# A twentieth place for expert weights, made of two pieces of reused memory

## What is computed

```python
def grouped_moe(h, router_w, router_bias, w1, w3, w2):   # h: 256 x 1024
    scores = sigmoid(h @ router_w)                       # 256 x 16
    gates = the top 2 experts of the best of 4 groups, normalised
    for e in range(16):                                  # w1, w3: 1024 x 512, w2: 512 x 1024
        a = silu(t @ w1[e]) * (t @ w3[e])
        y = y + gates[:, e:e + 1] * (a @ w2[e])
for i in range(2):
    x = x + g1 * mixer(h)          # h = modulate(rms_norm(x))
    x = x + g2 * grouped_moe(h)    # h = modulate(rms_norm(x))
return rms_norm(x, final_g)
```

## Time and profile before

| | us |
|---|---|
| median of 3 runs | 1049.43 |
| the profiled execution, its own time | 1049.43 |
| its span, first to last instruction | 1047.6 |
| TensorE busy | 997.7 (95%) |
| layer 0: first and last product of the experts | 324.30 to 539 |
| layer 1: first and last product of the experts | 821.41 to 1032 |

### The profile page before, as it was taken

The page is one execution under the profiler, slowest core; times in us unless marked ns, Lnnn a source line. Parts: engine busy times, 40 slices in busy tenths (PEclk is TensorE's granted clock), DMA queues, the critical chain, the costliest instruction groups (busy, mean ns, idle before and its releaser), DMA issues.

```text
span 1047.6 us, 18346 instructions
## 1 busy us (share of the span) xinstructions
PE 997.7 (95%) x7709; PEld 602.5 (58%) x7709; DVE 564.1 (54%) x1192; ACT 188.5 (18%) x395; POOL 40.5 (4%) x83
## 2 busy tenths in 40 slices
PE   7999999999999999998999999999999999999794
PEld 4788567557775344443358866765878534444321
DVE  4669794868786223361235779572758622233112
ACT  4031001311233031011131110122123301110102
POOL 2100100010000000000010010001000000000000
PEclk9999999999999999999999999999999999999997
DMA  9999856297976999999999884628875599999991
GB/s 310 387 381 332 280 172 232 85 330 278 418 292 224 421 386 421 420 421 421 420 388 375 291 311 162 222 71 288 301 286 213 200 420 420 421 419 421 421 417 71
DMA packets 91883, 333.94 MB, mean 319 GB/s; under 512 B 5740, under 2 KB 6059, under 8 KB 66965
## 3 DMA queue, kind: packets, MB, share of 16 engines
q1 hardware_dynamic: 87937, 323.56, 79.3%
q0 software_dynamic: 2976, 7.19, 2.3%
q10 hardware_dynamic: 884, 1.97, 0.6%
HBM read 329.47 MB, written 1.05 MB: 316 GB/s over the span
## 4 chain that ended last, share of the span: by engine, by line
PE 78%; DVE 8%; DMA 6%; SPq 3%; issue 2%; ACT 1%; DVEq 0%; ACTq 0%
PE bank L833 76%; DMA ring<-in_moe_w_dram 4%; SPq L732 3%; DMA ring<-in_w_ada_dram 2%; PE bank L1345 1%; PE bank L1121 1%; DVE wide L2018 0%; DVE area L2014 0%; DVE wide L1807 0%; PE bank L1174 0%; DVE x L2234 0%; PE bank L895 0%; DVE area L2233 0%; DVE area L2210 0%; DVE wide L2019 0%
## 5 line engine op out<-in xcount | busy, mean ns | idle before, releaser
L833 PE MATMUL bank<-ring,hT 128*32 128x512 f32 (+3 forms) x1808 | 283.8, 555 | 9.8 <-DMA ring<-in_moe_w_dram 7.0
L833 PE MATMUL bank<-hT,ring 128*32 128x256 f32 (+1 forms) x2112 | 211.8, 380 | 0.1
L833 PEld LDWEIGHTS bank<-ring,hT 128*32 128x32 f32 (+2 forms) x1808 | 120.8, 134 | 144.8 <-issue 139.6
L833 PEld LDWEIGHTS bank<-hT,ring 128*32 128x32 f32 (+1 forms) x2112 | 157.6, 132 | 52.2 <-issue 5.5
L833 PE MATMUL bank<-ring,area 128*32 128x512 f32 (+1 forms) x744 | 117.8, 566 | 1.3 <-ACT area L1681 0.9
L833 PE MATMUL bank<-area 32*64 32x64 f32 (+5 forms) x648 | 89.1, 363 | 0.0
L1807 DVE SCALAR_TENSOR_TENSOR area<-ring,wide,area 128x512 f32<-128x512 f32 x114 | 85.3, 748 | 2.7
L2442 DVE TENSOR_TENSOR area<-bank,area 128x512 f32<-128x512 f32 x14 | 9.7, 691 | 130.4 <-PE bank L833 130.4
L833 PE MATMUL bank<-wide,hT 128*32 128x512 f32 (+1 forms) x376 | 75.1, 574 | 0.0
L833 PEld LDWEIGHTS bank<-ring,area 128*32 128x32 f32 (+1 forms) x744 | 43.6, 120 | 53.7 <-issue 48.6
L833 PEld LDWEIGHTS bank<-area 32*64 32x64 f32 (+4 forms) x648 | 37.9, 145 | 45.7 <-issue 44.4
(11 more groups left out here) (300 smaller groups left out, 1077.7 us busy)
## 6 DMA issues: line engine op xcount, KB each, us to landing
ring<-in_moe_w_dram SPq DMA_DIRECT2D x136, 1024.0 KB, 16.5
ring<-in_w_ada_dram SPq DMA_DIRECT2D x24, 2048.0 KB, 15.0
ring<-in_w_in_dram SPq DMA_DIRECT2D x24, 2048.0 KB, 12.3
wide<-in_moe_w_dram SPq DMA_DIRECT2D x32, 1024.0 KB, 12.8
cst<-in_moe_w_dram SPq DMA_DIRECT2D x13, 1024.0 KB, 14.9
area<-in_moe_w_dram SPq DMA_DIRECT2D x11, 1024.0 KB, 19.5
ring<-in_w_out_dram SPq DMA_DIRECT2D x4, 2048.0 KB, 8.5
ring<-in_w_br_h_dram SPq DMA_DIRECT2D x4, 1536.0 KB, 6.7
```

The lines of the kernel that those rows point to most:

```text
L833: return pe.matmul(dst, lhsT, rhs, start=start, stop=stop, skip_group_check=True)
```

## The change

One place more, `PIECES`, for both layers. It has two pieces of 1024 columns: the upper half of `hT`, and `area` from `AREA - 6 * W` to `AREA - 4 * W`. To free the first, `hg` becomes the lower 1024 columns in one piece; to free the second, `selh`, `sil`, and half of `yS` go (their values are written into `sel`, `act` and `actT`). The new place is appended to the end of `free` at the start of each layer's experts. Its first block waits for `p_part`; a block in it is loaded by two DMAs of 512 KB (128 x 4 KB) in place of one of 1 MB (128 x 8 KB), both on the place's one semaphore, and `half_row` picks the piece for each row of weights. To have a semaphore left for it, two early ones (`s_rates` and `s_tab`) become one.

```diff
-        hg = hT[:, :, 0:P]
+        hT_flat = hT[:, :, :].rearrange("p k n -> p (k n)")
+        hg = hT_flat[:, 0:ND * P].rearrange("p (k s) -> p k s", k=ND)
...
-        selh = region(NT * P).rearrange("p (t s) -> p t s", t=NT)
         selT = region(SEQ)
-        sil = region(FE)
         act = region(FE)
-        actT = region(FE).rearrange("p (f s) -> p f s", f=NF)
-        yS = region(D)
+        actT_flat = region(FE)
+        actT = actT_flat.rearrange("p (f s) -> p f s", f=NF)
+        yS = (region(W), actT_flat)
...
-        assert cut[0] <= AREA - 4 * W
+        assert cut[0] <= AREA - 6 * W
+        halves += [(hT_flat[:, ND * P:2 * ND * P], area[:, AREA - 6 * W:AREA - 4 * W])]
...
                         if L + 1 == DEPTH:
                             free.insert(12, (ROWS, None))
+                        free.append((PIECES, None))
...
+                    if u == PIECES:
+                        landings[u] += 16
                     plan[key] = halves[u], u, landings[u] + 16, [old]
...
+        def half_row(space, k, f):
+            if isinstance(space, tuple):
+                per = 2 * W // f
+                space, k = space[k // per], k % per
+            return space[:, k * f:(k + 1) * f]
...
+                    elif u == PIECES:
+                        sp.wait_ge(p_part, (L + 1) * NT)
...
+                    rows, f = ((NF if m == 2 else ND) // 2, D if m == 2 else FE)
+                    spaces = dst if isinstance(dst, tuple) else (dst,)
+                    count = rows // len(spaces)
+                    for i, space in enumerate(spaces):
+                        first = half * rows + i * count
+                        sp.dma_start(space.rearrange("p (k f) -> p k f", f=f),
+                                     t[name][L, experts[e], :, :].rearrange(order, p=P)[:, first:first + count, :])\
+                          .then_inc(landing, 16)
...
                 def rates_to_all(l):
                     if l == 0:
-                        pe.wait_ge(s_rates, 16 * 2)
+                        pe.wait_ge(s_rates_tab, 16 * 3)
...
-                    sc.activation(sil, bank[0][:, :], ACT.Silu).then_inc(a_sil, 1)
+                    sc.activation(act, bank[0][:, :], ACT.Silu).then_inc(a_sil, 1)
...
-                    dv.tensor_tensor(act, bank[1][:, :], sil, ALU.mult).then_inc(v_act, 1)
+                    dv.tensor_tensor(act, bank[1][:, :], act, ALU.mult).then_inc(v_act, 1)
...
-                    link(dv.tensor_tensor(selg[b], selg[b], selh, ALU.add))
+                    link(dv.tensor_tensor(selg[b], selg[b], sel, ALU.add))
```

More of the change, by code:

```diff
@@ L77 @@
 EXTRA = 2 * RING
-TABLE, TAIL, ROWS = EXTRA + 4, EXTRA + 5, EXTRA + 6
+TABLE, TAIL, ROWS, PIECES = EXTRA + 4, EXTRA + 5, EXTRA + 6, EXTRA + 7
 LAST = {(0, EXTRA): 3, (0, EXTRA + 1): 3, (0, EXTRA + 2): 1, (0, EXTRA + 3): 1, (1, EXTRA + 2): 3, (1, EXTRA + 3): 3}
@@ L408, in trunk_kernel @@
         mask = cst[:, C_MASK:C_MASK + NT * KEYS].rearrange("p (t n) -> p t n", t=NT)
-        slot_in = [sem(f"slot_in{u}") for u in range(ROWS + 1)]
+        slot_in = [sem(f"slot_in{u}") for u in range(PIECES + 1)]
         p_ada = sem("p_ada")
@@ L420, in trunk_kernel @@
         s_taps = sem("s_taps")
-        s_rates = sem("s_rates")
+        s_rates_tab = sem("s_rates_tab")
         a_dec = sem("a_dec")
@@ L691, in _ @@
             for n in range(2):
-                sp.dma_start(rates[32 * n:32 * n + 1, :], t["decay"][n:n + 1, :]).then_inc(s_rates, 16)
+                sp.dma_start(rates[32 * n:32 * n + 1, :], t["decay"][n:n + 1, :]).then_inc(s_rates_tab, 16)
             for L, kind, b, half in loads:
@@ L730, in _ @@
                     name, order = ("moe_w1", "moe_w3", "moe_w2")[m], "(p k) f -> p k f"
-                    part = slice(half * (NF if m == 2 else ND) // 2, (half + 1) * (NF if m == 2 else ND) // 2)
-                    sp.dma_start(dst.rearrange("p (k f) -> p k f", f=D if m == 2 else FE),
-                                 t[name][L, experts[e], :, :].rearrange(order, p=P)[:, part, :]).then_inc(landing, 16)
+                    rows, f = ((NF if m == 2 else ND) // 2, D if m == 2 else FE)
[6 more added lines that the diff above has]
+                          .then_inc(landing, 16)
                 elif L == 0 and (kind == "rest" or (kind == "in" and b * 4 < AHEAD)):
@@ L927, in spectrum @@
                         pe.wait_ge(v_kt, (l + 1) * 12)
-                        pe.wait_ge(s_tab, 16)
+                        pe.wait_ge(s_rates_tab, 16 * 3)
                     else:
@@ L1328, in up @@
                                 pe.wait_ge(landing, value)
-                                ws.append(w.rearrange("p (k f) -> p k f", f=FE))
+                                ws.append(w)
                         if which == 0 and k == 0:
@@ L1358, in down @@
                             pe.wait_ge(landing, value)
-                            ws.append(w.rearrange("p (k f) -> p k f", f=D))
+                            ws.append(w)
                         for h in range(2):
@@ L1388, in scatter @@
                             mm(bank[2 + 2 * tt + h][:, :], selT[:, tt * P:(tt + 1) * P],
-                               yS[:, h * W:(h + 1) * W], True, True).then_inc(p_sc, 1)
+                               yS[h], True, True).then_inc(p_sc, 1)
                 def next_filter(s, spot):
@@ L1465, in _ @@
                                 last = mm(bank[2 + 2 * tt + h][:, :], selT[:, tt * P:(tt + 1) * P],
-                                          yS[:, h * W:(h + 1) * W], True, True)
+                                          yS[h], True, True)
                         last.then_inc(X["x_sc"], 1)
@@ L1479, in _ @@
                 sc.dma_start(x[:, tt, :], t["x"][0, tt * P:(tt + 1) * P, :]).then_inc(s_x, 16)
-            sc.dma_start(cst[:, C_CT:C_IC], t["cst"][:, C_CT:C_IC]).then_inc(s_tab, 16)
+            sc.dma_start(cst[:, C_CT:C_IC], t["cst"][:, C_CT:C_IC]).then_inc(s_rates_tab, 16)
             sc.wait_ge(p_rows, 2)
@@ L1680, in _ @@
                     sc.wait_ge(p_actT, n + 1)
-                    sc.activation(actT[:, :, :].rearrange("p f s -> p (f s)"), bank[0][:, :], ACT.Copy)\
+                    sc.activation(actT_flat, bank[0][:, :], ACT.Copy)\
                       .then_inc(a_actT, 1)
@@ L1717, in _ @@
                             sc.dma_start(w1, rows_in("moe_w3", 0)).then_inc(X["x_in"], 16)
-                            sc.activation(sil, bank[0][:, :], ACT.Silu).then_inc(X["x_sil"], 1)
+                            sc.activation(act, bank[0][:, :], ACT.Silu).then_inc(X["x_sil"], 1)
                             sc.wait_ge(X["x_up"], i * 4 + 3)
@@ L1724, in _ @@
                             sc.activation(selT, bank[4][:, 0:SEQ], ACT.Copy)
-                            sc.activation(actT[:, :, :].rearrange("p f s -> p (f s)"), bank[5][:, :], ACT.Copy)\
+                            sc.activation(actT_flat, bank[5][:, :], ACT.Copy)\
                               .then_inc(X["x_aturn"], 1)
@@ L1731, in _ @@
                 sc.activation(stat[:, 10, 0:1], eps[:, :], ACT.Sqrt)
-                used = ((sil, actT[:, :, :].rearrange("p f s -> p (f s)")), (hT[:, 0:4, P:SEQ], hT[:, 4:ND, P:SEQ]))
+                used = ((act, area[:, 0:W]), (hT_flat[:, 0:W], hT_flat[:, W:2 * W]))
                 for tt in range(NT):
@@ L2349, in select @@
                                          ALU.is_equal, ALU.mult)
-                        last = dv.tensor_scalar(selh[:, tt, :], iota, where[:, s, NT + tt:NT + tt + 1],
+                        last = dv.tensor_scalar(sel[:, tt, :], iota, where[:, s, NT + tt:NT + tt + 1],
                                                 token[:, 3, tt:tt + 1], ALU.is_equal, ALU.mult)
                     link(last)
-                    link(dv.tensor_tensor(selg[b], selg[b], selh, ALU.add))
+                    link(dv.tensor_tensor(selg[b], selg[b], sel, ALU.add))
                     dv.tensor_scalar(sel, selg[b], 0.0, None, ALU.is_gt).then_inc(v_sel, 1)
@@ L2450, in _ @@
                         dv.wait_ge(p_down, n * 2 + h + 1)
[L2451 removed]
+                        dv.tensor_tensor(yS[h], bank[6 + h][:, :], g2b[:, cols], ALU.mult).then_inc(v_yS, 1)
                 accumulate(STEPS - 1)
@@ L2479, in _ @@
                             dv.wait_ge(X["x_up"], i * 4 + 4)
-                            dv.tensor_tensor(act, bank[1][:, :], sil, ALU.mult).then_inc(X["x_act"], 1)
+                            dv.tensor_tensor(act, bank[1][:, :], act, ALU.mult).then_inc(X["x_act"], 1)
                             dv.wait_ge(X["x_down"], i * 2 + 2)
@@ L2483, in _ @@
                                 cols = slice(h * W, (h + 1) * W)
-                                last = dv.tensor_tensor(yS[:, cols], bank[6 + h][:, :], g2b[:, cols], ALU.mult)
+                                last = dv.tensor_tensor(yS[h], bank[6 + h][:, :], g2b[:, cols], ALU.mult)
                             last.then_inc(X["x_yS"], 1)
```

6 lines of the change are left out of this document (2 added, 4 removed).

## The result

The kernel after takes 1043.36 us, the median of 5 runs (1042.17 to 1043.95), against 1049.43 before: a ratio of 0.9939, with a 95% interval of 0.9925 to 0.9954. The forecast was 1045.1; the direction was right, and the gain is 6.1 us in place of 4.3. The profiled span is 1041.6 us (before 1047.6), so 6.0 us are gone from it.

A forecast was written before the change was run, and what follows sets the result against it. The late-starting weight stream was taken to bound both layers' experts. Span 1047.6 - 2.2 (layer 0) - 2.1 (layer 1) = 1043.3, so 1045.1 us of time; own range 1043.8 to 1046.3, overall range 1043.3 to 1049.6.

The forecast's parts named there:

- What bounds the kernel: Both layers' expert parts: the weight stream, full at 420 GB/s but started late, sets the end through the last block's landing.
- The new place: Each layer's expert stream: one block loads in idle time before the first release, so later blocks land 2.49 us earlier.
- Price of the pieces: Blocks loaded as two 4 KB-row transfers: 0.1 us each, bounds 0 and 0.23; 0.4 us at each layer's last block.
- Layer 0: Layer 0's experts: last block lands at 529.8 in place of 531.85; gain 2.2 us, or 2.4 with full clock.
- Layer 0's stall and the clock: TensorE in layer 0's step 5: stall 1.0 us in place of 3.19; 1.52 us of half clock may go, without mattering.
- Layer 1: Layer 1's experts: last block lands at 1022.85 in place of 1024.94, stalls about 4.6 us in total; gain 2.1 us.
- Layer 1's head: First 2 MB loads of layer 1 wait for releases a half product later, but the queue is full anyway: 0 us.
- The rest at 0: Other edits (hg in one piece, selh, sil and yS shared, joined semaphore): same instructions, waits already covered, 0 us.
- only one layer pays: Rival: layer 0's gain is waited out in layer 1's head; 1047.3 us, chance 0.14.
- it doesn't do what it says: Rival: SyncE's order keeps the new place's first block from landing before the first release; 1049.4 us, chance 0.06.
- the slower one: Rival: half transfers in the streams don't overlap, deciding from 0.62 us per block in pieces; 1063.6 us, chance 0.08.
- More than the sum: Rival: 4 KB rows cost nothing and layer 0 takes 2.4 us; 1044.5 us, chance 0.04 for below 1043.8.

The follow-up runs named there:

- a_split: Kernel after with every expert block, not only those in PIECES, loaded by two 512 KB transfers: 1056.57 us, ratio 1.0066.
- a_reads: Kernel after with three more rank reads on SyncE between the wait of layer 0's block 73 and its load: 1045.32 us, ratio 0.996.
- a_noplace: Kernel after with PIECES never handed out, all other edits kept: 1049.98 us, ratio 0.9997.
- a_only0: Kernel after with the new place handed out in layer 0 only: 1045.12 us, ratio 0.995.
- b_hoist: Kernel before with SyncE's reads of a step's ranks moved ahead of the release wait of its first block: 1048.74 us, ratio 0.9994.
- a_only1: Kernel after with the new place handed out in layer 1 only: 1048.4 us, ratio 0.9984.
- a_late: Kernel after with PIECES' first block waiting for the first release (first half product of step 0) in place of p_part: 1049.46 us, ratio 0.999.

## Why the prediction was right and wrong, point by point

- **What bounds the kernel**: right. Both layers end at the last landing, after too (528.40, then TensorE at 528.54; 1018.97, then 1019.11).
- **The new place**: right. Two issues at 313.64 and 314.01 (forecast 313.3), 14.65 and 14.6 us before the releases, landed by 324.0 and 814.6. The forecast had the block in by 321.6; in layer 0 small loads of GpSimd share the engines there, and 4 us to spare take it up.
- **Price of the pieces**: mis-sized, on the safe side. 0.1 us for a block was taken, 0.06 to 0.08 measured by a_split, and in the full queue of the kernel after seven of the eight blocks in pieces land 2.52 to 2.59 us behind the block before, the eighth, behind a late block, 2.39; most others 2.48 to 2.49. That is 0.2 to 0.3 us in a layer in place of 0.4.
- **Layer 0**: here a step failed. It is the sentence "so at each release the same number of transfers goes out, but each is one block further on". Up to step 3 it is true of the releases, and not of what stands between a release and a load: the reads of step 3's experts are bound to block 72, not to a place in the queue. Moving block 72 one release forward took 1.7 us of SyncE out of the one stretch in which the engines had nothing queued. The prediction asked what SyncE's second issue for the pieces costs (0.33 us, hidden) and never what the reads cost: they stand in it neither as a term nor as one put at 0. The rest of the step is right in size: 201.65 to 199.44 is 2.2 us, the 2.2 that were forecast. The missing term is the loss of 2.22 us that became 0.68, 1.54 us. The hand walk has a second slip, without a price: by the two kernels' `place_blocks()`, the twelve blocks of step 4 (loads 90 to 101) wait for the same releases as before, since one of the two `wide` places that leave after step 3 does so twelve blocks earlier, in step 4 in place of step 5. The queue was deep there: these blocks land some 2.5 us apart in both kernels, 10.7 to 25.9 us behind their issue.
- **Layer 0's stall and the clock**: no stall where 1.0 was forecast, from the same 1.54 us; with the reads back it is 0.80 (a_reads). Both halves take 7.08 us together, so the 5.16 us of one at half clock are gone as well. As argued, this didn't matter, since the last block is what is late next; TensorE waits 0.47 us for it. The 2.4 us that were given for the full clock had left out the 0.14 us from that landing (528.40) to TensorE's product (528.54); with them it is 2.2 either way.
- **Layer 1**: right, 2.35 us for a forecast of 2.1, stalls of 0.70 and 3.86 for 0.6 and 4. Of the 0.25 us more the cheaper pieces explain 0.1 to 0.2; the rest is within what these streams scatter: without the place they are 199.4 to 199.8 in a_noplace, a_only0 and b_hoist, with it 197.3 to 197.5 in six kernels.
- **Layer 1's head**: right. The second and third load start at 518.79 and 524.24 (forecast: by 520.4 and 524.1), no product of the head waits for a DMA there, and the distance from layer 0's last landing to layer 1's first release is 0.16 us shorter.
- **The rest at 0**: right (a_noplace).
- **The rivals**: "only one layer pays" fell by a_only0 and a_only1, "it doesn't do what it says" by the queue, the slower one by a_split. "More than the sum" came true in its size and not in its reason: it had put 1044.5 for cheap pieces and the full clock, and said that below 1043.8 "something unseen would have to help". That was the dry stretch.
- **The sum**: 2.2 + 2.1 forecast; 3.75 + 2.35 came, with 0.16 for the stretch between and 0.29 less for a later start: 5.97 of span. The range, 1043.3 to 1049.6, has the result at its very edge, and the forecast's own narrower one, 1043.8 to 1046.3, misses it by 0.4 us; the low ends had been set by the known terms alone. The trace before would have given the term: the prediction read the slices as full "in slices 14 and 16 to 20", and did not ask what happened in slice 15.

## What to carry to other kernels

Before a change makes a stream of loads deeper or earlier, go through the full part of the stream for stretches in which it isn't full, and see what the queue stood at there: a lead is lost at the next dry stretch unless one more transfer is issued in front of it, and closed gaps come on top of it. What an issuing engine does between a wait and the load behind it (here three reads of a register) is free as long as something is queued and costs its whole length where nothing is; it can be moved in front of the wait. The cost of splitting a transfer should be read from the cadence of queued transfers, not from the time that a lone one takes to land.

## What the runs showed of the hardware that was not expected

- Three `value_load` reads hold SyncE's queue for 1.67 us (b_hoist, a_reads), 0.56 for one.
- Two transfers of 512 KB with rows of 4 KB in place of one of 1 MB with rows of 8 KB cost 0.06 to 0.08 us in a full queue.
- A stall's length doesn't say by itself whether the clock falls behind it. In a_only1 a stall of 3.23 us in layer 0 is followed by the full clock, in a_late one of 2.18 us in layer 1 by half of it. TensorE's row and the stretch behind it (PEclk is the last but two), first of a_only1, then of a_late:

```profile
488.02 3.64 PE L850 MATMUL bank<-ring,hT 128*32 128x512 f32 x32 [3.23 <-DMA ring<-in_moe_w_dram]
```

```profile
488.00:491.00 3.00, 2.98 (x28) 1.12 (x32) 0.00 (x0) 0.00 (x0) 0.00 (x0) 1.00 1.02 423
```

```profile
977.78 1.05 PE L849 MATMUL bank<-hT 128*32 128x512 f32 x2 [2.18 <-DMA wide<-in_moe_w_dram]
```

```profile
977.80:979.80 2.00, 2.00 (x12) 0.70 (x16) 0.00 (x0) 0.00 (x0) 0.00 (x0) 0.51 1.00 418
```

In a_late a stall of 3.26 us stands 7.5 us ahead of the second. No run here was made to tell what decides it.

- Single blocks of a full stream land up to 1.6 us late, and the traces show what stands beside it. During each layer's stream in the kernel before, the DMA queues carry 13 transfers of 16 KB on a queue that the profile calls instruction. In the twelve profiled executions every block of a full stream, outside the dry stretch, that lands 0.6 us or more late does so 2.1 to 4.1 us after one of these transfers starts; most of the transfers are followed by no such block. In the kernel before the clearest case is the block that lands at 949.69, 1.26 us late. The queue between 946 and 949 (transfers, MB, share of 16 engines; 2.2% of 16 x 3 us is 1.06 us of one engine):

```profile
q8 instruction: 1, 0.02, 2.2%
```

This is part of the scatter of layer 1's stream (199.4 to 199.8 us without the place). That these transfers are the cause is not shown: no run moved one, and why most of them delay nothing stays open.
